# Sparse attention pair loop: one weight multiply for both heads, scores three pairs ahead, VectorE's round reordered

## What is computed

```python
def masked_softmax(s, mask):
    s = jnp.where(mask, s.astype(jnp.float32), NEG_INF)
    return jax.nn.softmax(s, axis=-1) * mask.astype(jnp.float32)
...
        s_c = jnp.einsum('bgrqd,bgnd->bgrqn', qc, k_cmp) * scale
        p_c = masked_softmax(s_c, cmp_end[None, :] <= t[:, None])
        o_c = jnp.einsum('bgrqn,bgnd->bgrqd', p_c, v_cmp)
...
        p_s = masked_softmax(s_s, tok <= t[:, None])
        o_s = jnp.einsum('bgrqk,bgqkd->bgrqd', p_s, v_s)
...
        p_w = masked_softmax(s_w, mask_w)
        o_w = jnp.einsum('bgrqk,bgkd->bgrqd', p_w, vw)
        g = g.transpose(2, 0, 3, 1).reshape(3, bsz, G, R, NSA_Q_CHUNK, 1)
        return g[0] * o_c + g[1] * o_s + g[2] * o_w
```

## Time and profile before

| | us |
|---|---|
| median of 3 runs | 1915.03 |
| the three runs | 1914.94, 1915.03, 1917.54 |
| the profiled execution | 1917.76 |
| its span, first to last instruction | 1916.0 |
| TensorE busy in it | 1839.4 (96%) |
| VectorE busy | 1247.2 (65%) |
| ScalarE busy | 917.1 (48%) |
| mean granted TensorE clock | 0.957 |

### The profile page before, as it was taken

The page is one execution under the profiler, slowest core; times in us unless marked ns, Lnnn a source line. Parts: engine busy times, 40 slices in busy tenths (PEclk is TensorE's granted clock), DMA queues, the critical chain, the costliest instruction groups (busy, mean ns, idle before and its releaser), DMA issues.

```text
span 1916.0 us, 33032 instructions
## 1 busy us (share of the span) xinstructions
PE 1839.4 (96%) x13492; PEld 1711.9 (89%) x13492; DVE 1247.2 (65%) x2120; ACT 917.1 (48%) x1585; POOL 113.3 (6%) x150
## 2 busy tenths in 40 slices
PE   6989998999899999999999999999999998999997
PEld 6979997888479998999979879999999997589997
DVE  6867668774777666766564338665676657557764
ACT  7545443542755454544454235444554545445442
POOL 1001004300010001000100020000000000000000
PEclk9999999997899999999998979999999999789999
DMA  4214555541025555555533214555455551025553
GB/s 153 78 44 165 187 185 202 187 144 45 1 89 185 184 193 193 182 176 176 190 108 101 76 66 144 172 174 191 138 190 185 195 188 62 27 89 200 186 198 122
DMA packets 76038, 276.35 MB, mean 144 GB/s; under 512 B 8496, under 2 KB 9520, under 8 KB 75760
## 3 DMA queue, kind: packets, MB, share of 16 engines
q1 hardware_dynamic: 75168, 270.57, 42.1%
q0 software_dynamic: 288, 2.30, 0.3%
q10 hardware_dynamic: 432, 1.38, 0.2%
HBM read 273.16 MB, written 1.05 MB: 143 GB/s over the span
## 4 chain that ended last, share of the span: by engine, by line
PE 88%; DVE 7%; ACT 3%; DMA 1%; issue 1%; DVEq 0%; SPq 0%; ACTq 0%
PE acc L1584 43%; PE mix L1584 19%; PE acc L1580 4%; PE mix L265 3%; PE acc L1581 2%; PE acc L1604 2%; DVE wl L1828 2%; DMA arrived<-in_w 1%; PE acc L1089 1%; PE acc L1350 1%; PE stat L1635 1%; PE acc L1658 1%; PE acc L1092 1%; PE mix L1658 1%; PE mix L1604 1%
## 5 line engine op out<-in xcount | busy, mean ns | idle before, releaser
L1828 DVE TENSOR_TENSOR wl<-arrived,wh 128x1024 fp32r<-128x1024 f32 x514 | 641.6, 1249 | 400.1 <-ACT wh L1704 388.3
L1704 ACT ACTIVATE wh<-arrived 128x1024 fp32r<-128x1024 f32 x514 | 542.0, 1058 | 585.1 <-DMA arrived<-in_w 584.7
L1584 PE MATMUL acc<-xh,wh 128*128 128x256 f32 (+1 forms) x1512 | 432.6, 286 | 0.0
L1584 PE MATMUL acc<-xh,wl 128*128 128x256 f32 (+1 forms) x1512 | 430.4, 285 | 0.0
L1584 PE MATMUL acc<-xl,wh 128*128 128x256 f32 (+1 forms) x1512 | 430.2, 285 | 0.0
L1584 PE MATMUL acc<-hx,wh 128*128 128x256 f32 (+1 forms) x1664 | 304.3, 284 | 0.0
L1584 PEld LDWEIGHTS acc<-xh,wh 128*128 128x128 f32 x1512 | 287.1, 190 | 5.9 <-issue 5.2
L1584 PEld LDWEIGHTS acc<-xh,wl 128*128 128x128 f32 x1512 | 287.2, 190 | 0.0
L1584 PEld LDWEIGHTS acc<-xl,wh 128*128 128x128 f32 x1512 | 286.1, 189 | 0.2
L1584 PE MATMUL mix<-xh,wh 128*128 128x256 f32 (+1 forms) x968 | 278.8, 288 | 2.3 <-DVE y L1447 1.4
L1584 PE MATMUL mix<-xh,wl 128*128 128x256 f32 (+1 forms) x968 | 277.1, 286 | 0.0
(11 more groups left out here) (408 smaller groups left out, 2339.7 us busy)
## 6 DMA issues: line engine op xcount, KB each, us to landing
arrived<-in_w SPq DMA_DIRECT2D x514, 512.0 KB, 3.3
scr<-in_cmp_w POOLq DMA_DIRECT2D x1, 2048.0 KB, 8.9
x<-in_x ACTq DMA_DIRECT2D x2, 544.0 KB, 8.1
out<-x SPq DMA_DIRECT2D x8, 128.0 KB, 1.8
par<-in_par ACTq DMA_DIRECT2D x1, 259.0 KB, 4.5
scr<-in_positions POOLq DMA_DIRECT2D x1, 128.0 KB, 7.1
scr<-in_cmp_w POOLq DMA_DIRECT2D x1, 32.0 KB, 9.2
scr<-in_w_gate POOLq DMA_DIRECT2D x1, 32.0 KB, 2.9
```

What stands on the lines that cost most here:

```text
L1584: ins = nc.tensor.matmul(bank(name, t)[:, 0:L - c], w_part[:, h.slot, w], v_part[:, k, c:], start=(k == 0 and w_part is wh and v_part is h ...
L1704: nc.scalar.activation(wh[:, h.slot, :], raw(h.slot), ACT.Copy).then_inc(w_hi, 1)
L1828: nc.vector.tensor_tensor(wl[:, h.slot, :], raw(h.slot), wh[:, h.slot, :].bitcast(F32), ALU.subtract).then_inc(w_lo, 1)
```

## The change

Three edits, all in the pair loop.

1. `normal` handles a pair at once: one reciprocal of the four columns of row sums, one multiply of these with the four gate values, then two tensor_tensor over both heads, 2x128 and 2x256 columns, with the factor broadcast along the row. `n_p` counts pairs, and `turned` waits for it accordingly.
2. TensorE issues the scores three pairs ahead: scores(2) before the loop and scores(p+3) in round p.
3. VectorE's round p is now multiply of pair p, minima of pair p+2, then attn_lo in odd rounds. The minima of pair 1 move ahead of the loop.

```diff
--- before.py
+++ after.py
@@ -661,7 +661,7 @@
                             ins.then_inc(n_s, 1)
 
             def turned(n):
-                pe.wait_ge(n_p, n + 1)
+                pe.wait_ge(n_p, n // 2 + 1)
                 if n >= 2:
                     pe.wait_ge(n_ptc, n - 1)
                 else:
@@ -699,6 +699,7 @@
 
             scores(0)
             scores(1)
+            scores(2)
             pe.wait_ge(n_vc, 4)
             for p in range(PAIRS + 1):
                 if p:
@@ -709,8 +710,8 @@
                         for h in range(2):
                             ins = nc.tensor.matmul(mix[j][DH * h:DH * h + DH, 0:SEQ], nvc[:, h, j, :], npct[:, h, 0, :], start=False, stop=True)
                         ins.then_inc(n_oc, 1)
-                if p + 2 < PAIRS:
-                    scores(p + 2)
+                if p + 3 < PAIRS:
+                    scores(p + 3)
                 if p < PAIRS:
                     turned(2 * p)
                     turned(2 * p + 1)
@@ -922,19 +923,22 @@
                                                          ALU.min, nstat[:, 2 * (n % 4) + qt:2 * (n % 4) + qt + 1])
                 ins.then_inc(n_min, 1)
 
-            def normal(n):
-                j, h, b = UNITS[n]
-                head = 8 * (j // 4) + 4 * h + j % 4
-                dve.wait_ge(n_exp, 2 * n + 2)
-                rec = nstat[:, 56 + 2 * (n % 2):58 + 2 * (n % 2)]
-                if n >= 2:
-                    dve.wait_ge(n_p, n - 1)
-                step(nc.vector.reciprocal(rec, nstat[:, 48 + 2 * (n % 4):50 + 2 * (n % 4)]))
+            def normal(p):
+
+                j, _, b = UNITS[2 * p]
+                head = 16 * (b + 1) + 8 * (j // 4) + j % 4
+                first = 2 * (p % 2)
+                dve.wait_ge(n_exp, 4 * p + 4)
+                rec = nstat[:, 56 + 2 * first:60 + 2 * first]
+                rec2 = rec.rearrange("p (h q) -> p h q", h=2)
+                if p >= 2:
+                    dve.wait_ge(n_p, p - 1)
+                step(nc.vector.reciprocal(rec, nstat[:, 48 + 2 * first:52 + 2 * first]))
+                step(nc.vector.tensor_tensor(rec2, rec2, ngate[:, :, head:head + 5:4].rearrange("p q h -> p h q"), ALU.mult))
                 for qt in range(2):
                     s = slice(P * qt, P * qt + P * (qt + 1))
-                    g = 16 * (b + 1) + head
-                    ins = nc.vector.tensor_scalar(nP[:, n % 4, s], nP[:, n % 4, s], rec[:, qt:qt + 1], ngate[:, qt, g:g + 1],
-                                                  ALU.mult, ALU.mult)
+                    v = nP[:, first:first + 2, s]
+                    ins = nc.vector.tensor_tensor(v, v, rec2[:, :, qt:qt + 1].to_broadcast([P, 2, P * (qt + 1)]), ALU.mult)
                 ins.then_inc(n_p, 1)
 
             dve.wait_ge(n_mask, 4)
@@ -943,17 +947,18 @@
             least(1)
             compressed(0)
             compressed(1)
+            least(2)
+            least(3)
             for p in range(PAIRS):
+                normal(p)
+                for n in (2 * p + 4, 2 * p + 5):
+                    if n < len(UNITS):
+                        least(n)
                 if p == 5:
                     attn_lo(dve, 0)
                     attn_lo(dve, 1)
                 elif p % 2 == 1 and p > 5:
                     attn_lo(dve, (p - 3) // 2)
-                for n in (2 * p + 2, 2 * p + 3):
-                    if n < len(UNITS):
-                        least(n)
-                normal(2 * p)
-                normal(2 * p + 1)
             attn_lo(dve, KD - 1)
             for m in range(KD):
                 tail(3, m, "nsa_out", BASE["nsa_out"] + m)
```

## The result

| | before | after |
|---|---|---|
| median of the runs shown with it, us | 1915.02 (5 runs) | 1904.6 (5 runs) |
| those runs, us | 1913.38 to 1917.54 | 1898.52 to 1908.8 |
| profiled execution / its span, us | 1917.76 / 1916.0 | 1905.67 / 1903.6 |
| first reciprocal of the loop to nsa_out, us | 62.28 | 55.30 |
| everything else in the span, us | 1853.7 | 1848.3 |

The ratio of the times, after over before, is 0.9948, 95% interval 0.9929 to 0.9968: 10 us faster, 6 to 14. With the executions that came with the experiments (then 23 of the changed kernel; 70 of the one before, without its first five), the means are 1906.2 and 1914.4 us: 8.2 us apart, standard error 1.0. So a good part of the surprise was probably not the change at all.

What follows compares the result with a forecast made beforehand. No engine's busy share but a circle of waits, closed by attn_lo heading VectorE's odd round, was taken as the bound. 3.7+2.7-0.5 = 5.9 us off the 1915.03 us median gave 1909.1 us, range 1906.8 to 1913.2.

Steps and rivals of the forecast that it cites:

- The circle: Pair loop: even transposes, copy, high part, low part, minima, multiply, odd transposes wait on each other; two rounds cost 7.70 us.
- The multiply: VectorE, per pair: both heads' weights ready after 1.44 us (1.3 to 1.6), before 0.86 and 1.64; VectorE gains 0.2 us a round.
- Slack of 1.4 us: Pair loop: the multiply ends 3.6 us after ScalarE's copies, TensorE wants it some 5 us after them.
- Part 3: Rounds 6 to 12, TensorE waiting for copies only: two rounds 6.48 us for 7.70, 3.7 us gained.
- Part 4, the tail: From the transposes of round 12 to nsa_out: 11.2 us instead of 13.93, 2.7 us gained.
- Part 5, the start: First transposes of the loop at 487.7 instead of 487.15 us: 0.5 us lost, scores(3) may cost 0.3 more.
- The earlier rise of the clock: Loop start: TensorE resumes 0.8 us earlier; if its clock rises as much earlier, 0.4 us comes back.
- Nothing later gives it back: After the loop: weight loads wait for TensorE's own progress and move with it, so the 5.9 us gain stays.
- 1 for the median: Whole time: the 1 us allowed for the median among the uncertainties behind the forecast's 1907 to 1911 us.
- A: Pair loop: ScalarE becomes the pacer, 3.5 us a round; gain 3.7 us, 1911.3 us, or 1912.5 with round 5 late; chance 0.16.
- B: Pair loop: the circle closes elsewhere, TensorE waiting for copies or minima; nothing that can be told, 1914 us; chance 0.10.
- C: Pair loop: the slower multiply stays on the path, 0.6 us lost in 15 rounds, 1924 us; chance 0.05.

Runs made afterwards that it cites:

- the 12 fresh runs: The changed kernel executed again with no edit, its third batch: mean 1908.1 us, median 1909.27 us, ratio 0.9972.
- transposes ahead: The changed kernel with TensorE's transposes of pair p issued before scores(p+3): median 1905.6 us, ratio 0.9942, loop 49.69 us.
- the two longer multiplies: The changed kernel with one or three idle 256-wide tensor_tensor in every pair's multiply: executed once each, 1911.19 and 1914.19 us.
- multiply alone: The kernel before with only the first edit, one multiply per pair, old VectorE order, scores two ahead: ratio 0.9999, loop 66.06 us.

## Why the prediction was right in the loop and wrong in its range

- **The circle.** Right. It was there, attn_lo at the head of the odd round closed it, and moving that one call brought 6.4 of 7.0 us.
- **The multiply.** Right: 684 ns for the term put at 700 (0.53 to 0.85 were the bounds), the first multiply 1.44 us as summed. It is off the path in the middle and alone brings nothing. A further column costs a tensor_tensor (684-425)/256 = 1.01 ns and a tensor_scalar 0.48, but in this order nobody waits for it. The Trainium skill ("VectorE: DVE Perf Modes", The perf-mode tier table) has tensor_scalar in float32 at twice the rate of tensor_tensor; these two slopes agree with it.
- **Slack of 1.4 us.** Right as a distance in time: 1.39 and 1.65 us in the two kinds of round. Wrong as what can be added: 0.34 us more is free in the middle, but 1.03 us, less than the slack, makes VectorE the bound. By its work the room is (6.32-5.3)/2 = 0.5 us a round, an estimate from the steps and the prediction's own account.
- **Part 3.** Mis-sized in one term. The step out of an odd round was put at 3.32 us, from an early round of 3.44 less 0.12 for a fourth transpose; it measured 3.16, so what the early rounds carry in addition costs 0.28. Rounds 6 to 12: 18.96 us, so 4.1 us gained for 3.7. The step from round 5 to 6, left out of the sum, gave 0.4 more.
- **Part 4, the tail.** 10.87 us for 11.2: 3.1 gained for 2.7.
- **Part 5, the start.** Loss of 0.9 us at the first transposes for 0.5: scores(3) ended at 485.5, 1.8 us behind the reciprocal, the late end of the 1.4 to 1.8 us (487.6 to 488.0) that was named. 0.3 of it came back by round 5. The earlier rise of the clock, which was set against the late scores, isn't there in the first profile: the loop begins with 6.0 us at the low level, 5.5 before. The three changed profiles have 6.0, 6.0 and 3.4, the two of before 5.5 and 6.0. What the Trainium skill ("TensorE: Matmul & The Clock Gate", What's actually happening) says of activity, that it releases the throttle, is neither shown nor refuted by them. By row: -0.89+0.21+0.08+0.40+4.13+3.06 = 6.99 us, the measured 6.98.
- **The median.** This is the step that failed. No run speaks against "Nothing later gives it back", but "1 for the median" was too small. Three runs within 2.6 us were taken for the spread of this program. The runs have a standard deviation of 3.7 us (before) and 4.5 (after), so a difference of two small medians is uncertain by some 3 us. The measured gain of 10.4 us consists of 7.0 of loop and 3.4 of the rest of the span, which the sum had at nothing. The loop's 1.1 us above the forecast would have left the time within the range, at 1908.0; the 3.4 took it out. An estimate of their cause: the five runs have 151.4 us at the low level in the mean, the 70 of before 158.2, and at 0.5 us each that is 3.4. As far as the 12 fresh runs tell, whose mean is 1908.1, it was chance. A range of 1903 to 1914 would have followed from the same case with that spread; that is said with the result known.
- **Rivals.** A didn't occur: TensorE waits for ScalarE's copies 0.25 us in each odd step of the middle and no more. ScalarE has no idle time left as soon as the rounds get shorter (transposes ahead). B and C are out by the 3.16 us steps and the two longer multiplies.

## What to carry to other kernels

When an engine that isn't the fullest waits long for a neighbour while the fullest one waits for it, look for what stands at the head of its round and doesn't belong to what the fullest one needs next; moving that one call behind the round's own work was worth nearly as much as the whole rewrite here. An operation may get slower in its latency if it leaves the path, and how much more it may take is measured by adding an idle instruction of known size; the time between its end and its use does not tell this, since its engine's work per round can run out first. Before setting a range, look at how the parts of the program that the change doesn't touch repeat: here they vary more from execution to execution than the change is worth, and a comparison of the changed stretch alone, in two profiles of each kernel, decides what a dozen timed runs leave open.

## What was not expected of the hardware

- TensorE's clock can fall inside a loop in which it works most of the time (52.5 of 66.1 us busy, multiply alone): within 2 us of the end of a 1.47 us wait, granted clock 0.5 and scores of 1.66 us instead of 0.93. It happened twice and cost 1.5 us each time. Two further waits of 1.48 us in the same loop were not followed by it.
- The same instructions behind the loop take 1359 to 1371 us, by how much of them falls to the 1.2 GHz level, 79 to 107 us.
- TensorE's busy time in the profile isn't its work: busy 25.1 of 26.5 us in the changed kernel, with two rounds at 6.32 us, and the same matmuls in another order take 5.35.
- A tensor_tensor of 2x256 columns with an operand broadcast along the row took 684 ns, (684-425)/256 = 1.01 ns for each column beyond the 256 of the narrower one. One of 1024 columns without a broadcast took 1249 ns, 1.07 ns a column from there, so no extra cost of the broadcast shows.
